# Six of the 24 modulation blocks of a two-layer kernel moved from the even layer's mixing stages to the odd layer's input projection and attention

## What is computed

```python
def even_layer(...):                                  # the odd layer likewise
    sh1, sc1, g1, sh2, sc2, g2 = ada_modulation(c[:, None, :], mod_w, mod_b)
    h = modulate(rms_norm(x, norm_mix), sh1, sc1) @ w_in
...
    x = x + g1 * (o_lat @ w_out)
    x = x + g2 * swiglu(modulate(rms_norm(x, norm_ffn), sh2, sc2), w1, w3, w2)
```

## Time and profile before

| | us |
|---|---|
| runs | 1889.14, 1891.86, 1888.60 |
| median | 1889.14 |
| the profiled execution | 1893.86 |
| its span | 1891.5 |
| even input projection | 43 to 166 |
| turn, Fourier part | 166 to 185 |
| even attention | 185 to 243 |
| dense stage | 306 to 688 |
| odd projection, turn, attention | 688 to 827 |
| experts | 891 to the end |

### The profile page before, as it was taken

The page is one execution under the profiler, slowest core; times in us unless marked ns, Lnnn a source line. Parts: engine busy times, 40 slices in busy tenths (PEclk is TensorE's granted clock), DMA queues, the critical chain, the costliest instruction groups (busy, mean ns, idle before and its releaser), DMA issues.

```text
span 1891.5 us, 25223 instructions
## 1 busy us (share of the span) xinstructions
PE 1808.7 (96%) x8938; PEld 1413.5 (75%) x8938; DVE 1240.5 (66%) x1297; ACT 1018.1 (54%) x1128; POOL 290.2 (15%) x552
## 2 busy tenths in 40 slices
PE   4999998999999989797999999999999999999998
PEld 2666545888888866456888888888888888888886
DVE  3242525243424236745998989989889899898997
ACT  3222834222222221453777777777677777777774
POOL 6886811020202025010000000000000000000000
PEclk8999999999999999896999999999999999999999
DMA  9797702131313150502998999999989999999994
GB/s 373 303 355 273 300 23 89 67 134 67 134 67 110 47 226 14 167 4 90 354 372 345 362 347 361 366 356 355 373 335 370 349 360 368 347 359 348 361 372 181
DMA packets 72501, 481.54 MB, mean 255 GB/s; under 512 B 7984, under 2 KB 11184, under 8 KB 17584
## 3 DMA queue, kind: packets, MB, share of 16 engines
q1 hardware_dynamic: 69872, 472.92, 65.9%
q0 software_dynamic: 1424, 5.51, 0.7%
q10 hardware_dynamic: 1136, 2.21, 0.4%
HBM read 473.29 MB, written 7.32 MB: 254 GB/s over the span
## 4 chain that ended last, share of the span: by engine, by line
PE 91%; DMA 3%; DVE 2%; ACT 2%; issue 1%; SPq 0%; POOL 0%; ACTq 0%; DVEq 0%
PE bank L1060 33%; PE bank L1074 16%; PE bank L793 12%; PE bank L763 4%; PE bank L822 3%; PE bank L810 3%; PE bank L858 3%; PE bank L643 2%; DMA ring<-in_ev_mod 2%; PE bank L581 2%; PE bank L1033 2%; PE bank L1043 1%; DMA ring<-in_od_mod 1%; PE bank L731 1%; PE bank L623 1%
## 5 line engine op out<-in xcount | busy, mean ns | idle before, releaser
L1832 DVE TENSOR_TENSOR rest<-ring,WR 128x2048 fp32r<-128x2048 f32 x336 | 758.3, 2288 | 79.9 <-ACT WR L1396 79.6
L1396 ACT ACTIVATE WR<-ring 128x2048 fp32r<-128x2048 f32 x336 | 632.2, 1917 | 47.5 <-DMA ring<-in_experts 46.8
L1060 PE MATMUL bank<-WR,xer 128*128 128x512 f32 x1792 | 581.1, 396 | 0.8 <-DVE s5v L1993 0.8
L1060 PEld LDWEIGHTS bank<-WR,xer 128*128 128x128 f32 x1792 | 337.9, 189 | 68.8 <-issue 0.9
L1060 PE MATMUL bank<-rest,xer 128*128 128x512 f32 x896 | 350.6, 391 | 0.0
L1074 PE MATMUL bank<-WR,heTr 128*128 128x512 f32 x896 | 281.9, 392 | 0.0
L793 PE MATMUL bank<-hTr,WR 128*128 128x512 f32 x672 | 207.4, 390 | 0.0
L1074 PEld LDWEIGHTS bank<-WR,heTr 128*128 128x128 f32 x896 | 168.3, 188 | 34.3
L1060 PEld LDWEIGHTS bank<-rest,xer 128*128 128x128 f32 x896 | 169.4, 189 | 32.6
L1074 PE MATMUL bank<-rest,heTr 128*128 128x512 f32 x448 | 174.5, 389 | 0.0
L1684 DVE TENSOR_TENSOR rest<-ring,WR 128x2048 fp32r<-128x2048 f32 (+2 forms) x38 | 80.3, 2115 | 123.8 <-ACT WR L1321 123.8
(11 more groups left out here) (339 smaller groups left out, 2165.7 us busy)
## 6 DMA issues: line engine op xcount, KB each, us to landing
ring<-in_experts SPq DMA_DIRECT2D x336, 1024.0 KB, 4.8
ring<-in_ev_mod SPq DMA_DIRECT2D x24, 1024.0 KB, 8.9
ring<-in_od_mod SPq DMA_DIRECT2D x24, 1024.0 KB, 7.9
ring<-in_ffn_up SPq DMA_DIRECT2D x22, 1024.0 KB, 6.8
ring<-in_ffn_down SPq DMA_DIRECT2D x12, 768.0 KB, 5.2
ring<-in_ev_in SPq DMA_DIRECT2D x8, 1024.0 KB, 6.5
ring<-in_ev_out SPq DMA_DIRECT2D x4, 1024.0 KB, 8.1
ring<-in_od_out SPq DMA_DIRECT2D x4, 1024.0 KB, 14.1
```

The costliest lines, as they stand in the source:

```text
L1060: mm = pe.matmul(bank[m % 2][:, :], xer[:, i, 4 * kh + k, :], w[j][:, 512 * k:512 * k + 512], start=(kh == 0 and k == 0 and x == 0), stop= ...
L1396: act.activation(part(0, h), ring[:, h % HALVES, :], ACT.Copy).then_inc(split_hi, 1)
L1832: dve.tensor_tensor(part(1, h), ring[:, h % HALVES, :], part(0, h).bitcast(F32), ALU.subtract).then_inc(split_lo, 1)
```

## The change

Blocks 0 to 17 stay in the even layer, in other places and other slots; blocks 18 to 23 go to the odd layer: behind tiles 8, 9 and 11 of its projection, into its turn at 0 and 3, and under step 2 of its attention. They are a fourth group with a bank of its own (6), a row in a part of `HT` and a turn into bank 7, in steps 3 and 4 of the odd attention. Their loads (18 to 22) stand behind the reload of scr_u and (23) behind the gathers of the lag table. As bank 6 is taken, `ODD_BANK` gives the last tiles other banks: tile 10 uses bank 7 and tile 11 bank 4. The buffer of `silc` is no longer free there, so ScalarE issues two DMAs of the conditioning ahead of the dense stage and makes their silu in its unit 5. Group 2 shrinks to 12 to 17, its row is copied in step 1 of the even attention and turned in step 2. The bias loads of heads 5 to 7 now stand behind those of the even output projection.

```diff
@@ -52,24 +52,33 @@
 UP_SLOTS, DOWN_SLOTS = FC // 2, 2 * len(FG)
 
 EARLY = ([("mod", s) for s in range(4)]
-         + [("in", 0), ("mod", 4), ("mod", 5), ("mod", 6), ("in", 1), ("mod", 7), ("mod", 8), ("mod", 9),
-            ("in", 2), ("mod", 10), ("mod", 11), ("mod", 12), ("mod", 13), ("in", 3)]
-         + [("mod", s) for s in range(14, 24)])
-EARLY_SLOT = [0, 1, 2, 0, 1, 2, 0, 2, 0, 2, 2, 1, 2, 1, 1, 0, 1, 0, 1, 2, 1, 2, 1, 2, 1, 2, 0, 1]
-UNDER_IN = {(0, 2): 4, (0, 3): 5, (0, 5): 6, (0, 7): 7, (5, 2): 8, (5, 7): 9, (7, 4): 10, (8, 7): 11, (9, 5): 12,
-            (10, 2): 13, (12, 0): 14, (13, 4): 15, (15, 0): 16}
-UNDER_TURN = {2: 17}
-UNDER_FOUR = {4: 18}
-UNDER_ATTN = {0: 19, 2: 20, 4: 21, 6: 22, 8: 23}
+         + [("in", 0), ("mod", 4), ("mod", 5), ("in", 1), ("mod", 6), ("mod", 7), ("mod", 8), ("in", 2),
+            ("mod", 9), ("mod", 10), ("mod", 11), ("in", 3)]
+         + [("mod", s) for s in range(12, 18)])
+EARLY_SLOT = [0, 1, 2, 0, 1, 2, 0, 2, 0, 1, 0, 1, 0, 2, 0, 2, 0, 1, 0, 1, 0, 1]
+UNDER_IN = {(0, 4): 4, (0, 6): 5, (4, 4): 6, (5, 5): 7, (6, 6): 8, (8, 3): 9, (9, 4): 10, (10, 4): 11, (12, 3): 12,
+            (13, 4): 13, (14, 4): 14, (15, 4): 15}
+UNDER_TURN = {1: 16}
+UNDER_FOUR = {}
+UNDER_ATTN = {0: 17}
 ROW_AT = max(UNDER_ATTN) + 1
 IN_BANK = (4, 5, 6, 2)
 ROW_JOB = 9
-S_MOD = [EARLY.index(("mod", s)) for s in range(24)]
+S_MOD = [EARLY.index(("mod", s)) for s in range(18)]
 S_IN_E = [EARLY.index(("in", n)) for n in range(4)]
-MOD_GROUPS = ((0, 4), (4, 12), (12, 24))
-S_OUT_E, S_FFN = 28, 30
+MOD_GROUPS = ((0, 4), (4, 12), (12, 18), (18, 24))
+LATE = 18
+ODD_TURN = {0: 21, 3: 22}
+ODD_ATTN = {2: 23}
+ODD_IN = {8: 18, 9: 19, 11: 20}
+LATE_SLOT = [2, 0, 2, 0, 1, 1]
+ODD_BANK = (4, 5, 6, 7, 4, 5, 6, 7, 4, 5, 7, 4)
+ODD_ROW = max(ODD_ATTN) + 1
+S_OUT_E, S_FFN = 22, 24
 S_IN_O = S_FFN + UP_SLOTS + DOWN_SLOTS
-S_OUT_O = S_IN_O + 4
+S_LATE = S_IN_O + 4
+S_OUT_O = S_LATE + 6
+S_MOD += [S_LATE + n for n in range(6)]
...
+        late_more = sb("late_more", [P, 84])
+        late_cond = [B[:, 11008:11260], late_more[:, :]]
+        silc_late = [x.rearrange("p (k s) -> p k s", s=42) for x in late_cond]
...
-        SLOTS = EARLY_SLOT + [i % RING for i in range(S_OUT_E, S_MOE)]
+        SLOTS = (EARLY_SLOT + [i % RING for i in range(S_OUT_E, S_LATE)] + LATE_SLOT
+                 + [i % RING for i in range(S_OUT_O, S_MOE)])
...
+                return mod_psum, LATE + 1 + i - S_LATE
...
-            return bank[(0, 3, 7)[g]]
+            return bank[(0, 3, 7, 6)[g]]
 
         def mod_rows(g):
-            return (mrow[:, 0, :], mrow[:, 1, :], rows[:, 0:512])[g]
+            return (mrow[:, 0, :], mrow[:, 1, :], rows[:, 0:512], HT[:, 3072:3584])[g]
 
         def mod_turn_bank(g):
-            return ((bank[1], 0), (bank[3], 0), (bank[6], 0))[g]
+            return ((bank[1], 0), (bank[3], 0), (bank[6], 0), (bank[7], 0))[g]
...
-                if i == S_MOD[14]:
+                if i == S_MOD[12]:
                     for h in range(3):
                         load_bias(h)
-                if i == S_MOD[22]:
-                    for h in range(5, NA_HEADS):
-                        load_bias(h)
-                if i == S_MOD[18]:
+                if i == S_MOD[15]:
                     for h in range(3, 5):
                         load_bias(h)
                 load(i, a["ev_in"][n] if what == "in" else a["ev_mod"][n] if n < 12 else a["od_mod"][n - 12])
             for n in range(2):
                 load(S_OUT_E + n, a["ev_out"][n])
+            for h in range(5, NA_HEADS):
+                load_bias(h)
...
+            for n in range(5):
+                load(S_LATE + n, a["od_mod"][6 + n])
             sp.wait_ge(lag_ready, 1)
...
+            load(S_LATE + 5, a["od_mod"][11])
...
-                        sp.wait_ge(*read(S_MOE - RING + u // 2))
+                        sp.wait_ge(*read((S_LATE + 5, S_OUT_O, S_OUT_O + 1)[u // 2]))
...
-                        mm = pe.matmul(o[32 * j:32 * j + 32, :], silc[:, c, at:at + 32], w[:, c, :],
+                        x = (silc[:, c, at:at + 32] if s < LATE else
+                             silc_late[c // 6][:, c % 6, at - 20:at + 12])
+                        mm = pe.matmul(o[32 * j:32 * j + 32, :], x, w[:, c, :],
                                        start=(s == lo and i == 0), stop=(s == hi - 1 and i == 1))
...
+                        elif r in ODD_ATTN:
+                            modulation(ODD_ATTN[r])
...
+                        if steps is ODD_STEPS and r == ODD_ROW + 1:
+                            pe.wait_ge(in_normed, 15)
+                            modulation_turn(3)
...
-                        pe.wait_ge(*((in_copied, i + 5) if i < 8 else (in_normed, i + 1)))
+                        pe.wait_ge(*((in_copied, i + 5) if i < 8 else (in_normed, i + 1 if i < 10 else i + 2)))
+                    if i == 11:
+                        pe.wait_ge(in_copied, 13)
...
+                    if i in ODD_IN:
+                        if ODD_IN[i] == LATE:
+                            pe.wait_ge(late_ready, 1)
+                            pe.wait_ge(in_normed, 11)
+                        modulation(ODD_IN[i])
...
+                    if jj in ODD_TURN:
+                        modulation(ODD_TURN[jj])
...
+                    pe.wait_ge(mod_ready, 2)
...
+            act.dma_start(late_cond[0], a["late"][:, 0:252]).then_inc(late_landed, 16)
+            act.dma_start(late_cond[1], a["late"][:, 252:336]).then_inc(late_landed, 16)
...
+                if u == 5:
+                    act.wait_ge(late_landed, 32)
+                    act.activation(late_cond[0], late_cond[0], ACT.Silu)
+                    act.activation(late_cond[1], late_cond[1], ACT.Silu).then_inc(late_ready, 1)
...
+                        if steps is ODD_STEPS and r == ODD_ROW:
+                            modulation_row(3)
...
+                        if r == ODD_ROW + 1:
+                            modulated(3, (3,))
...
-            modulated(2, (2, 3))
+            modulated(2, (2,))
```

More of the change, by code:

```diff
@@ L303, in build @@
         dve_step, act_step, pool_step = sem("dve_step"), sem("act_step"), sem("pool_step")
+        late_landed, late_ready = sem("late_landed"), sem("late_ready")
         cond_ready, mod_psum, mod_row, mod_turned, mod_ready = (
@@ L399, in read @@
                 return unit_done, 2 * (i - S_FFN + 1)
+            if i < S_LATE:
+                return in_psum, 16 + [4, 6, 8, 12][i - S_IN_O]
             if i < S_OUT_O:
-                return in_psum, 16 + [4, 6, 8, 12][i - S_IN_O]
+                return mod_psum, LATE + 1 + i - S_LATE
             return res_psum, 8 + 3 + i - S_OUT_O
@@ L857, in w_in_odd @@
                     for c in range(DC):
-                        mm = pe.matmul(bank[4 + i % 4][:, 0:w_], hT[:, c, t * P:(t + 1) * P], w[:, c // 4, c % 4, :],
+                        mm = pe.matmul(bank[ODD_BANK[i]][:, 0:w_], hT[:, c, t * P:(t + 1) * P], w[:, c // 4, c % 4, :],
                                        start=(c == 0), stop=(c == DC - 1))
@@ L1371, in _ @@
                 act.wait_ge(in_psum, 16 + i + 1)
-                ps = bank[4 + i % 4]
+                ps = bank[ODD_BANK[i]]
                 if n == 0:
@@ L1809, in _ @@
                        qn[:, t, 512 * (n - 1):512 * (n - 1) + w_].rearrange("p (h d) -> p h d", d=HD))
-                dve.tensor_tensor(dst, bank[4 + i % 4][:, 0:w_].rearrange("p (h d) -> p h d", d=HD),
+                dve.tensor_tensor(dst, bank[ODD_BANK[4 + i]][:, 0:w_].rearrange("p (h d) -> p h d", d=HD),
                                   hss[:, 0:heads].unsqueeze(2).to_broadcast([P, heads, HD]),
@@ L2295, in host_layout @@
     arrays = {"cond": cond.reshape(P, 62 * DC), "vec": v, "cst": constants(), "dft": dft_constants(), "rpb": rpb,
-              "s5b": bb.reshape(P, 2 * UNITS * S5_DIM), "s5c": cc.reshape(P, 2 * UNITS * S5_DIM)}
+              "late": np.ascontiguousarray(cond[:, :, 20:62]).reshape(P, 42 * DC), "s5b": bb.reshape(P, 2 * UNITS * S5_DIM), "s5c": cc.reshape(P, 2 * UNITS * S5_DIM)}
     def slots(w, cols):
```

## The result

The changed kernel is slower: 1897.97 us median of 9 runs (1896.68 to 1902.84), beside 1893.15 us (1888.60 to 1894.22) of the kernel before in 9 runs. The ratio of the two kernels is 1.0033, 95% interval 1.0022 to 1.0044, or 6.2 us; the medians alone lie 4.8 us apart, which is inside that interval. The forecast was -0.5 us, and the range ended at 1895.5 us. Nine runs put the kernel before 4 us above the three that the forecast started from, so the ratio is the number to explain.

The account below looks back on a forecast made before the run. TensorE, 91% of the chain, was taken as the bound, though not always in the odd stretch. Even side -12.0 us plus odd side +11.5 gave -0.5 on 1889.1, so 1888.6 us; 8 in 10 within 1882.0 to 1895.5.

Parts of the forecast that it names:

- Items 1 to 3: Even projection: one block and its load waits go, -6.3 us; query/key turn: 0; Fourier part: its block goes, -1.85 us.
- Item 4: Even attention: the blocks of steps 2, 4, 6 and 8 go, -4.8 us in sum.
- Item 5: Even attention: biases of heads 5 to 7, queued behind the output projection's 4 MB, come late: +0.9 us (0 to +3).
- item 12: Odd attention: the 4.3 us wait may drop the clock to half for 3.5 us: +1.7 us (0 to +4).
- Items 6 to 9: Odd projection and turn: blocks 18 to 22 added, attention starts near 774.2 us instead of 769.2, step 2's scores 4.0 later.
- item 9: Odd turn and first two attention steps: clock should stay at 2.4 GHz, so step 2's scores come 4.0 us later, not 5.0.
- Item 10: Odd attention step 2: block 23, loaded behind the gathers, makes TensorE wait 4.3 us; +8.7 us with items 6, 8 and 9.
- Item 11: Odd attention steps 3 and 4: the modulation row, its turn and its sums add +1.1 us (+0.3 to +2).
- C: Slower rival, even attention: biases come late, heads 5 and 7 each hold ScalarE 2 us or more; +3.5, 1892.1 us, chance 0.10.
- B: Slower rival, odd attention: clock falls in block 23's wait and stays down for long; +6 us, 1894.6 us, chance 0.18.
- A: Faster rival, odd attention: gathers clear the queue sooner, block 23 costs only its own time; total -6.4, 1882.7 us, chance 0.17.
- D: Slower rival: even projection keeps its waits, another block starved by the slot order; the 4.5 us stay, 1893.1 us, chance 0.07.

Follow-up runs that it names:

- experiment 1: Changed kernel with the bias loads of heads 5 to 7 ahead of the even output projection's loads again: 1896.65 us, ratio 1.0008 to the kernel before.
- experiment 4: Kernel before, with the matmuls of blocks 20 to 23 in the even attention cut from 512 to 8 columns: 1887.64 us, ratio 0.9972.
- experiment 2: Changed kernel with block 23 in ring slot 2 and its load ahead of the lag table's write and gathers: 1888.22 us, ratio 0.9981.
- experiment 3: Changed kernel with the edits of experiment 1 and experiment 2 together: 1886.18 us, ratio 0.9962 to the kernel before.
- version 3: The kernel of experiment 3, the changed kernel with both load-order edits: 1886.18 us, ratio 0.9962.
- experiment 6: Version 3 with blocks 13 to 17 under even attention steps, biases of heads 5 to 7 ahead of blocks 16 and 17: 1883.54 us, ratio 0.9947.
- experiment 7: Version 3 with the bias loads of heads 3 and 4 also behind block 17's load: 1886.36 us, ratio 0.9969 to the kernel before.

## Why the prediction was wrong

**Items 1 to 3, right.** The even projection gave 6.4 us (6.3 forecast), turn and Fourier part 1.4 (1.85, less the 0.4 allowed for uncovered copies). The cover of block 15 is as thin as said, and fails at times (experiment 1).

**Item 4, right.** Four blocks out of the even attention are worth 4.3 us (experiments 1 and 4), 4.8 forecast.

**Item 5, the first failed step.** The place, the cause and the asking time (17.0 us behind the attention's start, 17.2 forecast) were right. Head 5's bias landed 15.5 us after the first issue of the 4 MB and not 13.5, since the last half ahead of it took 13.5 us where the earlier trace rows had 11.3; why it took longer is open. So VectorE waited 3.0 us instead of 0.7. Behind that wait TensorE idled 3.23 us, the granted clock was 0.50 from 202.0 to 205.4 us, and the two steps behind it ran longer: 4.2 us in all against 0.9. The sum had no term for the clock there at all, though item 12 had one for the same kind of wait.

**Items 6 to 9, right in size.** Up to the odd attention +4.7 us, 5.0 forecast; step 2's scores came 6.6 us after the first ones instead of 7.6, the 1.0 us of item 9. The turn ran at full clock as item 9 said (granted 1.00 from 757.0 to 766.5 us), but then the clock did fall, at 768.6 us, to 0.50 until 775.4, which "should stay at 2.4" had excluded; the scores of steps 1 and 2 took 2.08 us. What makes it fall there is open: the traces of experiments 1 and 2 have the same two waits ahead of it, 0.83 and 1.56 us, and stay at 1.00.

**Item 10, the second failed step.** The mechanism was right: one wait on block 23, because its load stands behind the gathers. Counted from the table's write, TensorE asked for the block after 17.9 us (16.7 forecast) and it landed after 23.1 (21.0 forecast). The 2.1 us are the write's own landing, 4.9 us for 2.0, less 0.8 by a faster last leg: the step took the write's time from an empty queue, and the change itself had put block 22's 2 MB in front of it. The wait was 5.2 us, not 4.3.

**Item 12, too small.** It had 1.7 us for the clock; block and weighted sum at half clock took 785.79 - 780.38 = 5.4 us for some 2.9, so 2.5 us. The stretch ahead of the wait, which no item had, cost another 1.2 (steps 1 and 2 beside experiment 2's). Together 5.2 + 2.5 + 1.2 = 8.9 us, where items 10 and 12 had 4.3 + 1.7 = 6.0; experiment 2 took away 9.0. That the wait alone is enough for the clock shows in the trace of experiment 1, at full clock up to it (granted 1.00 until 779.6 us, then 0.50 to 786.5):

```profile
775.67 1.13 PE L719 MATMUL bank<-HT 64*128 64x512 f32 x4 [1.52 <-ACT S L1289]
782.97 2.78 PE L601 MATMUL bank<-ring,B 128*32 128x512 f32 x10 [6.18 <-DMA ring<-in_od_mod]
786.54 1.09 PE L756 MATMUL bank<-S,B 128*64 128x128 f32 x16
```

**Item 11, right.** From step 3 on the attention took 47.8 us for 46.9, and 47.8 again in experiments 2 and 3: 0.9 us for 1.1.

**The rivals.** C is the one that happened, at 4.2 us instead of 3.5, on top of an odd attention that was 3.1 us dearer. I had treated the rivals as alternatives, with one range end for each; C and a dear block 23 are independent and add: -0.5 + 3.3 + 3.1 = +5.9 us, beside 6.2 us measured. From the forecast's start, 1889.1 us, that makes 1895.0, still inside the range; what put the median outside it as well is the start, which nine runs put 4 us higher. B's sign came at its edge, half clock for 5.3 us behind the wait, but for 2.5 us and not 7.7. A was excluded as argued: the gathers stayed slow, and block 23 landed 12 to 13 us behind its issue. D did not come in this trace; experiment 1's wait for block 15 is of its kind.

**The tail, not forecast and not from the change.** From the odd output projection to the experts the nine traces took 59.6, 60.0, 60.9, 62.6, 63.2, 63.3, 63.3, 63.3 and 63.4 us, and the kernel before itself is among the long ones while experiment 4, with its code there, is among the short ones. The first 33.4 us of it are the same in all nine. The rest, here the kernel before and then the changed one (length, busy PE, PEld, DVE, ACT, POOL, clock, DMA, GB/s), differs by 2.28 us, of which 2.25 are TensorE's busy time, at a lower granted clock:

```profile
861.04:890.85 29.81, 24.04 (x138) 23.40 (x139) 14.90 (x54) 13.24 (x19) 0.31 (x1) 0.61 0.07 27
```

```profile
867.96:895.49 27.53, 21.79 (x139) 21.31 (x139) 14.87 (x54) 13.49 (x19) 0.31 (x1) 0.69 0.07 29
```

In all nine traces TensorE is idle for 5.7 to 5.8 us there, and its busy time goes from 20.5 to 24.3 us with the clock between 0.70 and 0.61. The experts took 999.5 to 1001.4 us in the nine, without an order by version. So one pair of spans, 3.5 us apart, says less than the medians: without the last two stretches the two traces are 6.9 us apart.

## What to carry to other kernels

A load that is moved in a queue changes the landing of everything behind it: price each small transfer behind it by what is then in front, not by its time in an empty queue. Here a wait on TensorE's path cost more than its length, since the work behind it ran at half clock (3.2 us of waiting cost 4.2, and 6.2 cost 8.0): put that term beside every wait of the sum, not beside the largest alone. And rivals in different stages are not alternatives: add them when the range is made. Last, take the start of a forecast from enough runs: three were 4 us off, beside an effect of 5 to 6.

## What the runs showed of the hardware

- A write of 240 KB took 2.0, 4.9 and 9.7 us to land with none, one and two blocks of 2 MB on the way ahead of it: 2.9 us more for the first block and 4.8 for the second.
- With the same idle time of 0.83 and 1.56 us ahead of them, the scores of the odd attention's step 1 took 2.08 us in the changed kernel, version 3 and experiments 6 and 7, and 1.13 us in experiments 1 and 2: the clock fell in some executions only.
- Five blocks with their matmuls cut to 8 columns saved 3.0 us of 9.3: the granted clock was 0.50 from 757.8 to 774.9 us, where with the blocks it had been 1.00 up to 768.6, and at half behind the wait in both.
- The same code of 60 us lasted between 59.6 and 63.4 us, with a granted clock of 0.70 to 0.61 in its second half.
- GpSimd reached the same instruction at 139.3 to 144.6 us in the five traces with the same code up to there, after waits for its own DMA writes.
